# A decoder layer on one core: gated expert outputs added onto the residual in DRAM by an indirect accumulating DMA, in place of a buffer that is gathered at the end

## What is computed

```python
# x: (2048, 1024) residual, h = rmsnorm(x, norm_moe)
gates = g_gate[:, None] * softmax(top_v)            # two per token
eid   = g_sel[:, None] * 8 + top_i                  # two experts per token
# the 4096 (token, expert) pairs sorted by expert, each expert padded to blocks of 128
y_e   = (silu(h @ w1[e]) * (h @ w3[e])) @ w2[e]     # D_EXPERT = 512
x     = x + sum_k gates[:, k] * y_of_pair[:, k]
out   = rmsnorm(x, norm_final)
```

## Time and profile before

| | |
|---|---|
| median of 3 runs | 3216.15 us (3213.57 to 3225.51) |
| span of the profiled execution | 3216.4 us |
| PE busy | 2769.5 us (86%), 14217 matmuls |
| DVE busy | 1733.3 us (54%) |
| ACT busy | 1284.8 us (40%) |
| POOL busy | 199.6 us (6%) |
| DMA | 463.98 MB, 144 GB/s over the span |
| route | 2063 to 2122 us |
| run_experts | 2122 to 3122 us |
| combine | 3122.6 to 3216.4 us |

### The profile page before, as it was taken

How to read it: one execution, slowest core, us unless ns; L and a number is a source line. 1 busy time by engine, 2 the same in 40 slices (tenths; PEclk the granted TensorE clock), 3 DMA queues, 4 the chain that set the end, 5 groups by cost and what they waited for, 6 DMA issues and landing times. The chain is left out here.

```text
span 3216.4 us, 46286 instructions
## 1 busy us (share of the span) xinstructions
PE 2769.5 (86%) x14217; PEld 2251.1 (70%) x14219; DVE 1733.3 (54%) x2349; ACT 1284.8 (40%) x2332; POOL 199.6 (6%) x300
## 2 busy tenths in 40 slices
PE   6999699499999997997899999559878899999970
PEld 5888488377777775776678888447666688878750
DVE  3222255399999994220333333365666655555537
ACT  3222233166666663110322222135666655455432
POOL 0000011300000000000000000000000000000013
PEclk9999799799999998998999999769899899999985
DMA  4222311542222203223312221146888867676649
GB/s 150 92 91 85 134 52 59 190 144 60 46 46 49 46 3 111 103 96 131 130 56 78 80 79 67 43 166 227 299 296 297 298 242 240 231 244 230 237 174 368
DMA packets 215356, 463.98 MB, mean 144 GB/s; under 512 B 38656, under 2 KB 71936, under 8 KB 213248
## 3 DMA queue, kind: packets, MB, share of 16 engines
q1 hardware_dynamic: 192544, 380.34, 35.8%
q0 software_dynamic: 15984, 58.20, 4.9%
q10 hardware_dynamic: 6768, 24.64, 2.0%
HBM read 363.50 MB, written 99.61 MB: 144 GB/s over the span
## 5 line engine op out<-in xcount | busy, mean ns | idle before, releaser
L1850 DVE TENSOR_TENSOR moe_w_lo<-moe_raw,moe_w_hi 128x1024 f32 (+1 forms) x256 | 305.2, 1223 | 173.0 <-ACT moe_w_hi L1795 157.4
L1795 ACT CAST moe_w_hi<-moe_raw 128x1024 f32 (+1 forms) x256 | 261.9, 1050 | 184.8 <-DMA moe_raw<-in_w 154.5
L759 PE MATMUL stick_o_ps<-stick_v,stick_weight_t 128*128 (+1 forms) x2176 | 291.6, 273 | 2.7 <-DVE stick_weight_t L829 1.3
L759 PEld LDWEIGHTS stick_o_ps<-stick_v,stick_weight_t 128*128 128x128 f32 x2176 | 267.7, 191 | 28.1 <-DVE stick_weight_t L829 16.3
L778 ACT ACTIVATE stick_leave<-stick_z_ps 128x512 f32<-128x512 f32 (+3 forms) x320 | 171.3, 535 | 237.0 <-PE stick_z_ps L740 131.8
L813 DVE TENSOR_TENSOR_SCAN stick_left<-stick_leave,stick_left 128x512 f32<-128x512 f32 x192 | 245.4, 1278 | 0.0
L52 PE MATMUL moe_g_ps<-moe_w_hi,moe_x_hi 128*128 x376 | 165.7, 441 | 64.8 <-DVE moe_w_lo L1850 48.8
L1881 DVE TENSOR_TENSOR moe_w_lo<-moe_raw,moe_w_hi 128x1024 fp32r<-128x1024 f32 x128 | 153.5, 1223 | 87.8 <-ACT moe_w_hi L1839 87.2
L750 PE MATMUL stick_t_ps<-all_ident,stick_weight 128*128 128x128 f32 x1088 | 182.1, 283 | 21.5 <-DVE stick_weight L822 16.6
L822 DVE TENSOR_TENSOR stick_weight<-stick_weight,stick_left 128x512 f32<-128x512 f32 (+3 forms) x320 | 188.0, 588 | 0.0
L750 PEld LDWEIGHTS stick_t_ps<-all_ident,stick_weight 128*128 128x128 f32 x1088 | 118.5, 141 | 85.9 <-DVE stick_weight L822 74.8
(11 more groups left out here) (280 smaller groups left out, 6003.6 us busy)
## 6 DMA issues: line engine op xcount, KB each, us to landing
moe_raw<-in_w SPq DMA_DIRECT2D x512, 256.0 KB
moe_raw<-in_w SPq DMA_DIRECT2D x128, 512.0 KB, 5.1
y_scratch<-moe_y ACTq DMA_DIRECT2D x47, 512.0 KB, 5.4
y_scratch<-stick_zeros POOLq DMA_DIRECT2D x31, 512.0 KB
qkv_xs<-in_x SPq DMA_DIRECT2D x16, 512.0 KB, 4.7
qt_scratch<-qkv_q_t SPq DMA_DIRECT2D x16, 512.0 KB, 3.2
kt_scratch<-qkv_k_t SPq DMA_DIRECT2D x16, 512.0 KB, 3.4
gmlp_xs<-in_x SPq DMA_DIRECT2D x16, 512.0 KB, 3.6
```

The costliest lines, as they stand in the source:

```text
L759: last = nc.tensor.matmul(o_ps[:, i % 2, 0:head_dim], weight_t[:, w % 2, b], v_sb[:, bass.ds((g % 2) * tiles * head_dim + (c * per + b) * ...
L1795: nc.scalar.copy(w13_hi[:, w13_at(e, i)], raw[:, i % RING]).then_inc(w13_cut, 1)
L1850: nc.vector.tensor_tensor(w13_lo[:, w13_at(e, i)], raw[:, i % RING], as_f32(w13_hi[:, w13_at(e, i)]), ALU.subtract).then_inc(w13_ready, 1)
```

## The change

- The 31 stores of zeros in attend_stick go, and ybuf with them.
- x2 gets 128 more rows (`spill`), one for each lane, where empty slots are added. route clears them (POOL memset, SP store).
- route carries a second value through the one-hot product, the gate, so that slot_gates comes out beside slot_tokens, and forms slot_rows, the row of x2 for each slot (the token, or a spill row). in_block and slot_ps are twice as wide. Gates and dests leave route no more.
- run_experts: ScalarE multiplies y by the slot's gate as it copies it from PSUM. POOL adds y_sb onto the rows of x2 by an indirect DMA with an add (`scatter(b)`), after the scatter before has landed, so that two blocks never add at the same time. In POOL's loop gather(b + 2) stands ahead of scatter(b).
- combine becomes finish_norm: x2 is loaded in 16 DMAs, four in flight, normed tile by tile in place and stored from ScalarE's queue.

```diff
 def attend_stick(...)
-                nc.gpsimd.memset(zeros[:], 0.0).then_inc(zeroed, 1)
-                pool.wait_ge(zeroed, 1)
-                with pool.Fori(0, spare.shape[0] // P) as b:
-                    pool.dma_start(spare[bass.ds(b * P, P), :], zeros[:]).then_inc(spare_cleared, 16)
-                pool.wait_ge(spare_cleared, 16 * (spare.shape[0] // P))
...
 def route(...)
+                nc.gpsimd.iota(lane[:], [[0, 1]], base=tokens + 1, channel_multiplier=1, allow_small_or_imprecise_dtypes=True).then_inc(built, 1)
+                nc.gpsimd.iota(token[:], [[P, tiles]], base=1, channel_multiplier=1, allow_small_or_imprecise_dtypes=True).then_inc(built, 1)
...
                 nc.gpsimd.memset(ones[:], 1.0).then_inc(built, 1)
-                pool.wait_ge(built, 5)
+                nc.gpsimd.memset(zeros[:], 0.0).then_inc(zeroed, 1)
+                pool.wait_ge(built, 6)
                 nc.gpsimd.affine_select(out=before[:], in_=ones[:], compare_op=ALU.is_gt, fill=0.0, base=0,
...
-                link(nc.vector.tensor_copy(dests[:], dest[:]))
...
                     nc.vector.tensor_scalar(in_slot[:, n % 2], lanes[:], dest_part[:, 1, k, t:t + 1], None, ALU.is_equal).then_inc(cut, 1)
-                    nc.vector.tensor_scalar(in_block[:, n % 2], block_no[:, :, 0], dest_part[:, 0, k, t:t + 1], token[:, t:t + 1],
-                                            ALU.is_equal, ALU.mult).then_inc(cut, 1)
+                    for part, value in enumerate((token[:, t:t + 1], gates[:, k, t:t + 1])):
+                        nc.vector.tensor_scalar(in_block[:, n % 2, part], block_no[:, :, 0], dest_part[:, 0, k, t:t + 1], value,
+                                                ALU.is_equal, ALU.mult).then_inc(cut, 1)
                 dve.wait_ge(slotted, pairs)
-                link(nc.vector.tensor_copy(slot_tokens[:], slot_ps[:]))
+                link(nc.vector.tensor_copy(slot_gates[:], slot_ps[:, 1]))
+                link(nc.vector.tensor_scalar(slot_no[:], slot_ps[:, 0], -1.0, None, ALU.add))
+                link(nc.vector.tensor_scalar(slot_tokens[:], slot_no[:], 0.0, None, ALU.max))
+                link(nc.vector.tensor_scalar(empty_row[:], slot_no[:], 0.0, lane[:, 0:1], ALU.is_lt, ALU.mult))
+                link(nc.vector.tensor_tensor(slot_rows[:], slot_no[:], empty_row[:], ALU.add))
+
+            @block.sync
+            def _(sp):
+                sp.wait_ge(zeroed, 1)
+                sp.dma_start(spill, zeros[:]).then_inc(spill_cleared, 16)
+                sp.wait_ge(spill_cleared, 16)
...
 def run_experts(...) 
+                def scatter(b):
+                    if not isinstance(b, int):
+                        pool.wait_ge(stored, 16 * b)
+                        pool.sem_inc(y_free, 1)
+                    pool.wait_ge(y_scaled, b + LEAD + 1)
+                    nc.gpsimd.tensor_copy(rows_now[:], slot_rows[:, bass.ds(b, 1)]).then_inc(rows_listed, 1)
+                    pool.wait_ge(rows_listed, b + 1)
+                    pool.sem_inc(rows_seen, 1)
+                    nc.gpsimd.indirect_dma_start(out=x2, out_offset=bass.IndirectOffsetOnAxis(ap=rows_now[:].bitcast(U32), axis=0),
+                                                 in_=y_sb[:], in_offset=None, compute_op=ALU.add).then_inc(stored, 16)
+
                 used = blocks_in_use(pool)
                 gather(0)
-                with pool.Fori(1, used + 1) as b:
-                    gather(b)
+                gather(1)
+                gather(2)
+                scatter(0)
+                with pool.Fori(1, used) as b:
+                    gather(b + 2)
+                    scatter(b)
+                pool.wait_ge(gathered, 16 * used + 32)
+                pool.wait_ge(stored, 16 * used)
+                pool.sem_inc(all_stored, 1)
...
                         act.wait_ge(y_done, b)
-                        act.wait_ge(stored, 16 * b)
+                        act.wait_ge(y_free, b)
                         for part in range(2):
-                            last = nc.scalar.copy(y_sb[:, part * BANK:(part + 1) * BANK], y_ps[:, part * BANK:(part + 1) * BANK])
-                        last.then_inc(y_free, 1)
-                        act.wait_ge(y_free, b + 1)
-                        act.dma_start(ybuf[bass.ds((b - 1) * P, P), :], y_sb[:]).then_inc(stored, 16)
+                            last = nc.scalar.activation(y_sb[:, part * BANK:(part + 1) * BANK], y_ps[:, part * BANK:(part + 1) * BANK],
+                                                        ACT.Copy, scale=slot_gates[:, bass.ds(b - 1, 1)])
+                        last.then_inc(y_scaled, 1)
...
-                        pe.wait_ge(y_free, b)
+                        pe.wait_ge(y_scaled, b + LEAD - 1)
...
 def finish_norm(...)
+                for n in range(tiles):
+                    if n >= GROUP:
+                        sp.wait_ge(x_loaded[n % GROUP], 16 * (n // GROUP))
+                    sp.dma_start(xs[:, n], x2[n * P:(n + 1) * P, :]).then_inc(x_loaded[n % GROUP], 16)
...
+                def store(n):
+                    act.wait_ge(done, n + 1)
+                    act.dma_start(out[n * P:(n + 1) * P, :], xs[:, n]).then_inc(stored[n % GROUP], 16)
+
+                for n in range(tiles):
+                    act.wait_ge(x_loaded[n % GROUP], 16 * (n // GROUP + 1))
+                    if n >= 2:
+                        act.wait_ge(squared, n - 1)
+                    nc.scalar.activation(junk[:, n % 2], xs[:, n], ACT.Square, accum_out=stat[:, 0, n:n + 1]).then_inc(squared, 1)
+                    if n >= 2:
+                        store(n - 2)
```

More of the change, by code:

```diff
@@ L606, in _, with attend_stick @@
                 mix(tiles - 1)
-def attend_stick(nc, qt, kt, v, ident, ident_bf, above, yb, spare):
+def attend_stick(nc, qt, kt, v, ident, ident_bf, above, yb):
     heads, parts, tokens = qt.shape
@@ L1478, in route @@
     blocks = slot_tokens.shape[1]
+    tokens = tiles * P
     LOW, LOWER = -1e30, -3e30
@@ L1933, in _, with finish_norm @@
                 rounds(pe, step)
-def combine(nc, x2, ybuf, gates, dests, gain, half, out):
-    tokens, width = x2.shape
+def finish_norm(nc, x2, gain, half, out):
+    tokens, width = x2.shape[0] - P, x2.shape[1]
     tiles = tokens // P
     GROUP = 4
-    groups = tiles // GROUP
     with ExitStack() as stack:
@@ L1977, in _ @@
             def _(pool):
-                def gather(g, parity, first):
-                    nc.gpsimd.tensor_copy(now[:, parity], dests[:, :, bass.ds(g * GROUP, GROUP)]).then_inc(listed, 1)
-                    pool.wait_ge(listed, g + 1)
-                    pool.sem_inc(list_seen, 1)
-                    for i in range(GROUP):
-                        if not first:
-                            pool.wait_ge(added, GROUP * (g - 1) + i + 1)
-                            pool.sem_inc(list_seen, 1)
-                        for k in range(2):
-                            nc.gpsimd.indirect_dma_start(out=ys[:, i, k], out_offset=None, in_=ybuf,
-                                                         in_offset=bass.IndirectOffsetOnAxis(ap=now[:, parity, k, i:i + 1].bitcast(U32), axis=0)
-                                                         ).then_inc(y_loaded[i], 16)
@@ new lines, in _ @@
+                for n in range(tiles):
+                    act.wait_ge(x_loaded[n % GROUP], 16 * (n // GROUP + 1))
[4 more added lines that the diff above has]
+                        store(n - 2)
+                store(tiles - 2)
+                store(tiles - 1)
+                for i in range(GROUP):
+                    act.wait_ge(stored[i], 16 * tiles // GROUP)
@@ L2015, in _ @@
                 dve.wait_ge(gains_loaded, 16)
-                def add(g, i):
-                    n = g * GROUP + i
-                    if i == 0:
-                        dve.wait_ge(x_loaded[g], 16)
-                    dve.wait_ge(y_loaded[i], 32 * (g + 1))
-                    for k, into in enumerate((first_added, added)):
-                        if k:
-                            dve.wait_ge(first_added, n + 1)
-                        nc.vector.scalar_tensor_tensor(out=tile_of(g, i), in0=ys[:, i, k], scalar=gates[:, k, n:n + 1], in1=tile_of(g, i),
-                                                       op0=ALU.mult, op1=ALU.add).then_inc(into, 1)
@@ L2057, in set_constants, with scale @@
+                def scale(n):
+                    dve.wait_ge(rooted, n + 1)
+                    nc.vector.scalar_tensor_tensor(out=xs[:, n], in0=xs[:, n], scalar=stat[:, 2, n:n + 1], in1=gains[:],
+                                                   op0=ALU.mult, op1=ALU.mult).then_inc(done, 1)
+                mean(0)
+                for n in range(1, tiles):
+                    mean(n)
+                    scale(n - 1)
+                scale(tiles - 1)
 def set_constants(nc, ident, half, ident_bf, above):
@@ L2111, in build_trunk @@
                 yb = m.sbuf("yb", [P, tiles, half_width])
```

(3 more changed lines are left out.)

135 lines of the change are left out of this document (43 added, 92 removed).

## The result

The kernel after takes 3263.16 us (median) against 3217.21 us, a ratio of 1.0129 with a 95% interval of 1.0108 to 1.015. It is slower by 1.3%; 3184 us had been forecast, and the range ended at 3245. Its profiled execution spans 3263.2 us, so as before terms from the trace can be set beside the medians.

A forecast was written before the change was run, and what follows sets the result against it. It took late loads beside zeros, a serial router chain, weight waits then TensorE in the experts, and closing-stage bytes as bounds; 3216.4 - 17 - 42 + 7 + 8 + 10 + 2 = 3184 us, range 3155 to 3245.

The forecast's parts named there:

- Zeros, -17: Start of attend_stick: without the stores of zeros the first load completes at 617 us, not 634.9; gain 17 us (12 to 19).
- Rival D: First head's load in attend_stick stays late through its 256-byte pieces; gain falls from 17 to 5 us, 3196 us; chance 0.05.
- Closing stage, -42: Combine: bytes fall from 34.1 to 17.3 MB, so about 52 us remain; gain 42 us (36 to 45).
- Router, +7: Router: a third VectorE operation and wider matmul per pair, plus a memset and small operations; loss 7 us (4 to 12).
- DMA work, +8: Expert stage: the scatter's 0.52 MB of extra reads cost 1.55 us in 18 weight-bound blocks; loss 8 us, at most 28.
- ScalarE's relief: Weight-bound expert blocks: the store leaves ScalarE's queue, saving the cast of h 0.57 us over 18 blocks; up to 10 us.
- Pool's queue, +10: TensorE-bound expert blocks: gather behind the scatter lands late in some 13 of 27 blocks, 0.8 us each; loss 10 us (0 to 27).
- Rival A: Experts: gather late everywhere, excess over 9.1 us from scatter issue to landing paid at 27 blocks; 3286 us; chance 0.15.
- Handover, +2: Experts to closing stage: barriers wait for the last scatter, whose scaling may wait for the one before; loss 2 us (0 to 6).

The follow-up runs named there:

- before_late_zeros: The kernel before with Pool's 31 stores of zeros waiting until the first head's keys and values are loaded; 3204.53 us, ratio 0.9951.
- plain_first: The kernel after with the gather issued ahead of the scatter and the scatter's add left out (outputs overwrite rows); 3157.52 us, ratio 0.9798.
- gather_first: The kernel after with gather(b + 3) placed ahead of scatter(b) in Pool's loop; 3195.2 us, ratio 0.9915.
- pool_wait: The kernel after without the scatter's DMA; Pool stands idle until the next block's gate product ends, then issues the gather; 3278.8 us, ratio 1.0177.
- pool_wait_thin: pool_wait with every weight load after the first expert's cut to a quarter of its columns or less; 3140.23 us, ratio 0.9752.
- pool_busy_once: The kernel after with one Pool fill of a tile in place of the scatter's DMA; 3165.31 us, ratio 0.9829.
- pool_busy: The kernel after with three Pool fills of a tile in place of the scatter's DMA; 3274.68 us, ratio 1.0184.

## Why the prediction was wrong, point by point

- *Zeros, -17:* right (-17.3, and -18.0 by itself in before_late_zeros). Rival D, a load that stays late, did not happen.
- *Closing stage, -42:* -47.4, just beyond the better bound of 45. The start and end around the transfer were set at 8 us for 44 us of transfer; with 17.3 MB in 46.3 us hardly any of it appeared.
- *Router, +7:* +7.9. Two pairs went from 1.32 to 1.69 us; 0.35 had been taken.
- *DMA work, +8:* the mechanism was right, the size was not. It cost 23.5 us in 14 blocks, 1.7 us each, inside the bound of 28. The step that failed is the choice near the low end: a ring of full chunks does not cover DMA work where the weights set the pace. The price of a scatter was taken from its bytes (1.55 us); the packets show 1.8 us (2.1 by the scatters that stand alone), with a like result. The rule of the Trainium skill ("Collectives: The Full Stack", section "The bandwidth ceiling: the fold count and why AG ≠ RS ≠ AR"), an add at half the rate of a copy, is borne out in direction: 0.34 us a packet against 0.145, a factor of 2.3, and 0.38 against 0.14 for a scatter alone. Of ScalarE's relief, up to 10 us of gain as the bound below zero, no run shows more than 3 us: plain_first, which has it without the add, takes 339.1 us where the kernel before takes 342.3.
- *Pool's queue, +10:* this is the step that decided, and it failed by a factor of seven: 65.4 + 7.1 = 72.5 us. Its parts: Pool needed 3.9 us from the copy to the gather's issue instead of 3.5 (the scatter's issue took 1.60 us, not the 0.97 of a gather), and 4.7 in every other block, where VectorE's subtractions held Pool's copy up; the steps had been added up from lines in which Pool ran undisturbed. The landing was taken from the old place, "near the minimum of 4.2 us" in quiet blocks, and it was 7.7 in the median and never below 6.1. The windows of the earlier trace rows average over 10.3 us; the gather's own few microseconds are the full part of them, since SP's loads are released around then. In the block shown above the DMA share from the gather's issue to its landing is 0.94 and 0.97. So 26 of 27 blocks paid, not 13: 0.9 us each in the 12 where the gather was issued 3.9 us behind the copy, 2.0 us each in the 15 where it was 4.7 or more. Last, no loss of clock had been reckoned with: 20.4 of the 65.4 us are matmuls that run slower between the waits.
- *Rival A* is what happened, with a chance of 0.15 on record. From the scatter's issue to the gather's landing it took 2.6 to 3.4 us plus 7.7, an excess of 1.2 to 2.0 us over the 9.1 that were left, in 26 of 27 blocks. Its price of 92 us at an excess of 3.4 was too high, its mechanism (the loop closes on itself) right. What delayed the landing was mainly another queue's loads (7.7 us with them, 5.7 without), and the scatter ahead added 0.8 us (5.7 against 4.9, with thin loads).
- *Handover, +2:* +8.0, above the bound of 6. The barrier was taken to wait for the landing; it waits for Pool's DRAIN as well, which ended about 11.3 us after the scatter's issue whether the scatter had landed after 6.2 us (gather_first) or 3.3 (plain_first).

## What to carry to other kernels

When a transfer is moved, its time of travel is moved too: read which other queue's packets are released in the microseconds ahead of the new moment of issue, not the mean DMA share around it. Behind a wait, issue first what somebody waits for and then what nobody waits for: here the order of two calls is worth 68 us. In this kernel an accumulating scatter costs 0.2 us each where the DMA engines have room and 2 us each where they are the bound; and the last DMA of a stage, issued by Pool, held the next stage back for 10 to 12 us.

## What was not expected of the hardware

- A packet of the accumulating scatter takes 0.34 to 0.38 us of a DMA engine, one of the plain scatter 0.14, and the issue holds Pool for 1.60 us instead of 0.99.
- A gather issued behind weight loads of another queue sends its first packet after 2.3 to 3.8 us (median 3.5, pool_wait) instead of 1.64 to 1.80 in 25 of 27 cases with thin loads.
- The issue of a gather on Pool lasts 0.96 us with VectorE idle and up to 2.04 us beside VectorE's subtraction of two operands in SBUF (pool_wait_thin, pool_busy_once, after).
- The next stage starts 10.4 us after Pool's last DMA was issued when it is a gather, and 12.1 to 12.3 us when it is a scatter, with the add (landed after 6.2 us) or without it (landed after 3.3).
- With waits of up to 3.8 or 4.8 us once a block TensorE's granted clock fell from 0.99 to 0.96, 0.95 and 0.94 (after, pool_busy, pool_wait), and the same matmuls of 27 blocks took 516, 527 and 529 us instead of 496. In pool_wait_thin, whose waits are 2.7 us at most, it stayed at 0.99. That the waits are the cause was not tried by itself.
